# A ring of twelve slots for the expert weights, six of them in buffers of the dense stages

## What is computed

```python
mod = silu(c) @ w_ada + b_ada                      # shifts, scales, gates
h = rmsnorm(x, norm1) * (1.0 + sc1) + sh1
z = h @ w_in                                       # pool group, gates B and C, value
pool_out = pool_mixer(u, ...)                      # windows 2/4/8/16, then w_pool
conv_out = conv_mixer(gate_b, gate_c, val, ...)    # three taps
x = x + g1 * (concatenate([pool_out, conv_out]) @ w_out)
h2 = rmsnorm(x, norm2) * (1.0 + sc2) + sh2
logits = h2 @ w_router + b_router                  # 32 experts, top 4, softmax over the four
g = minimum(xb @ w_gate[e] + b_gate[e], 7); u = clip(xb @ w_up[e] + b_up[e], -7, 7)
y = ((u + 1.0) * g * sigmoid(1.702 * g)) @ w_down[e] + b_down[e]
x = x + g2 * sum over the four experts of gate * y; rmsnorm(x, final_norm)
```

## Time and profile before

| | us |
|---|---|
| median of 3 runs | 1441.77 |
| lowest and highest | 1438.84, 1443.11 |
| the profiled execution's own time | 1442.45 |
| its span in the profile | 1440.7 |
| PE busy | 1292.0 |
| DVE busy | 464.9 |
| POOL busy | 304.0 |
| ACT busy | 132.0 |

### The profile page before, as it was taken

How to read it: one execution, slowest core, us unless ns; L and a number is a source line. 1 busy time by engine, 2 the same in 40 slices (tenths; PEclk the granted TensorE clock), 3 DMA queues, 4 the chain that set the end, 5 groups by cost and what they waited for, 6 DMA issues and landing times. The chain is left out here.

```text
span 1440.7 us, 44313 instructions
## 1 busy us (share of the span) xinstructions
PE 1292.0 (90%) x19889; PEld 1004.1 (70%) x19889; DVE 464.9 (32%) x708; ACT 132.0 (9%) x270; POOL 304.0 (21%) x335
## 2 busy tenths in 40 slices
PE   4999979657999999999999999999999999999710
PEld 2777734424987887877888788788779887788600
DVE  1210153442233342322333433323323333233244
ACT  3100101200010000000010000000100000001002
POOL 4002200152012211121122111221221112211226
PEclk9999989767999999999999999999999999999955
DMA  9726820235999999999999999999999999999461
GB/s 325 220 88 231 328 105 30 89 129 218 392 410 410 408 408 410 411 412 404 410 407 403 410 398 408 406 413 417 405 409 406 411 411 412 409 413 407 194 259 69
DMA packets 88792, 479.31 MB, mean 333 GB/s; under 512 B 15235, under 2 KB 24939, under 8 KB 39061
## 3 DMA queue, kind: packets, MB, share of 16 engines
q1 hardware_dynamic: 73842, 456.59, 79.3%
q0 software_dynamic: 11840, 20.64, 3.9%
q10 hardware_dynamic: 3075, 1.58, 0.5%
HBM read 468.41 MB, written 17.84 MB: 338 GB/s over the span
## 5 line engine op out<-in xcount | busy, mean ns | idle before, releaser
L1385 PE MATMUL acc<-raw,ht 128*32 128x256 f32 x12288 | 723.6, 382 | 24.7 <-DVE ht L1219 11.5
L1385 PEld LDWEIGHTS acc<-raw,ht 128*32 128x32 f32 x12288 | 565.0, 111 | 175.0 <-issue 67.8
L1385 PE MATMUL acc<-raw,at 128*32 128x256 f32 x6144 | 347.6, 380 | 2.8 <-DVE y_sb L1234 2.8
L1385 PEld LDWEIGHTS acc<-raw,at 128*32 128x32 f32 x6144 | 275.4, 110 | 60.8 <-issue 4.7
L1120 POOL DMA_INDIRECT expert_rows<-y_sb,y_idx x96 | 118.0, 1230 | 366.6 <-ACT y_idx L1158 325.6
L1109 POOL DMA_INDIRECT rows<-h_rows,row_next x90 | 91.6, 1018 | 462.6 <-DVE row_next L1214 443.2
L1266 DVE TENSOR_TENSOR g_sb<-acc,bias_gu 128x768 f32<-128x768 f32 x32 | 30.6, 958 | 326.1 <-PE acc L1385 326.1
L1155 ACT ACTIVATE y_sb<-y_sb,table 128x256 f32<-128x256 f32 x96 | 41.9, 499 | 929.8 <-DVE y_sb L1234 929.8
L862 PE MATMUL acc<-h_t,raw 128*128 128x288 f32 (+1 forms) x512 | 120.5, 398 | 1.1 <-DVE h_t L623 1.1
L862 PEld LDWEIGHTS acc<-h_t,raw 128*128 128x128 f32 x512 | 98.5, 193 | 23.0 <-issue 2.8
L1225 DVE STREAM_TRANSPOSE at<-a_sb 128x768 f32<-128x768 f32 x32 | 51.2, 1601 | 148.8 <-PE acc L1385 148.8
(11 more groups left out here) (219 smaller groups left out, 499.9 us busy)
## 6 DMA issues: line engine op xcount, KB each, us to landing
raw<-in_w_gate SPq DMA_DIRECT2D x128, 1024.0 KB, 7.5
raw<-in_w_up SPq DMA_DIRECT2D x128, 1024.0 KB, 6.1
raw<-in_w_down SPq DMA_DIRECT2D x128, 1024.0 KB, 7.6
raw<-in_w_ada SPq DMA_DIRECT2D x24, 1024.0 KB, 14.2
raw<-in_w_in SPq DMA_DIRECT2D x8, 1024.0 KB, 14.6
picked<-expert_rows SPq DMA_DIRECT2D x4, 2048.0 KB, 9.0
raw<-in_w_out SPq DMA_DIRECT2D x4, 1024.0 KB, 5.0
x_sb<-in_x_prompt SPq DMA_DIRECT2D x1, 2048.0 KB, 9.6
```

The source lines that it names most:

```text
L1385: mm = pe.matmul(out_[b][q * TB:(q + 1) * TB, :], x[:, b, k, :], w[:, kk, q * CW:(q + 1) * CW], start=(k == 0), stop=(k == KT - 1))
```

## The change

There are two rings of six slots, each one buffer: `ring_a`, the old one, and `ring_b`, new, 6 x 2048 floats per partition. The experts' weights use all twelve slots (`XSLOTS`), chunks 0 to 5 in `ring_b` and 6 to 11 in `ring_a`, with twelve semaphores of their own; the dense chunks stay in `ring_a`. Tiles of the dense stages that had buffers of their own now lie in `ring_b`: `pooled`, `wsum` and `wpool_sb` in its first two slots, `uext`, `uext_s`, `vext`, `vext_s` and `g1_bc` in the others. `picked` and `pair` of the last block lie there too. SP issues the first twelve expert chunks in the dense block, where the tiles beneath are done with: 6 and 7; then 0 and 1; stores of h2; 2 to 5; a store; 8 to 11; the last store. In the expert stage a load waits for the product twelve before it.

```diff
+XSLOTS = 12
-        raw = [keep(f"raw{s}", [P, SLOT_F]) for s in range(SLOTS)]
+        ring_a = keep("raw", [P, SLOTS * SLOT_F])
+        raw = [ring_a[:, s * SLOT_F:(s + 1) * SLOT_F] for s in range(SLOTS)]
+        ring_b = keep("raw_b", [P, SLOTS * SLOT_F])
+        slot_of = [(ring_b, s) for s in range(SLOTS)] + [(ring_a, s) for s in range(SLOTS)]
+        def slots(n, count=1):
+            ring_, s = slot_of[n]
+            return ring_[:, s * SLOT_F:(s + count) * SLOT_F]
+        slot_loaded = [sem(f"slot_loaded{s}") for s in range(XSLOTS)]
...
+        pooled = done_first([GR, NTOK])
+        wsum = [done_first([PAST + SEQ]) for i in range(2)]
+        wpool_sb = done_first([GR, P])
+        held_at[0] = 2 * SLOT_F
+        uext = done_first([GR, PAST + SEQ])
+        uext_s = done_first([GR, DEC_B, PAST + DEC_T])
+        vext = done_first([GR, CPAST + SEQ])
+        vext_s = done_first([GR, DEC_B, CPAST + DEC_T])
+        g1_bc = done_first([D])
...
             def first(n):
-                kind, e, c = FIRST_STREAM[n]
-                sp.wait_ge(*used(DENSE_CH - SLOTS + n))
-                sp.dma_start(raw[n][:, :].rearrange("p (k n) -> p k n", k=KC), expert_src(kind, e, c))\
-                    .then_inc(raw_loaded[n], 16)
-            for n in range(SLOTS - OUT_CH):
-                first(n)
-            for t in range(TT):
+                kind, j = expert_chunk(n % (2 * MCH))
+                sp.dma_start(as_rows(slots(n)), expert_src(kind, n // (2 * MCH), j)).then_inc(slot_loaded[n], 16)
+            def store(t):
                 sp.wait_ge(h_ready, TT + t + 1)
                 sp.dma_start(h2_dram[t * P:t * P + norm_rows(t), :], h_row[t % 2][0:norm_rows(t), :])\
                     .then_inc(h2_stored[t % 2], 16)
-            for n in range(SLOTS - OUT_CH, SLOTS):
+            for n in range(SLOTS, XSLOTS - OUT_CH):
+                sp.wait_ge(*used(DENSE_CH - XSLOTS + n))
                 first(n)
+            sp.wait_ge(tp_full, TP["pm_s"] + 1)
+            for n in range(2):
+                first(n)
+            for t in range(3):
+                store(t)
+            sp.wait_ge(tp_full, TP["so0"] + 1)
+            sp.wait_ge(new_packed, 4)
+            sp.wait_ge(x1_ready, PT)
+            for n in range(2, SLOTS):
+                first(n)
+            store(3)
+            for n in range(XSLOTS - OUT_CH, XSLOTS):
+                sp.wait_ge(*used(DENSE_CH - XSLOTS + n))
+                first(n)
+            store(4)
...
                 def load(i, c):
-                    n = pos(i, c)
-                    s = ring(i, c, SLOTS)
-                    kind = "gud"[c // MCH]
-                    sp.wait_ge(mm_done, n - (SLOTS - 1))
...
+                    n, s = pos(i, c), slot_at(i, c)
+                    kind, j = expert_chunk(c)
+                    sp.wait_ge(mm_done, n - (XSLOTS - 1))
+                    sp.dma_start(as_rows(slots(s)), expert_src(kind, i - (kind == "d"), j))\
+                        .then_inc(slot_loaded[s], 16)
-                for c in range(SLOTS, 2 * MCH):
-                    load(0, c)
-                with sp.Fori(1, E) as i:
+                for c in range(XSLOTS - 2 * MCH, NCH):
+                    load(1, c)
+                with sp.Fori(2, E) as i:
...
-                    pe.wait_ge(raw_loaded[ring(i, c, SLOTS)], loaded_value(i, c))
-                    w = raw[ring(i, c, SLOTS)][:, :].rearrange("p (k n) -> p k n", k=KC)
+                    pe.wait_ge(slot_loaded[slot_at(i, c)], loaded_value(i, c))
+                    w = as_rows(slots(slot_at(i, c)))
...
-            picked = [sb(f"picked{b}", [P, 2, 2, D]) for b in range(2)]
-            pair = [sb(f"pair{b}", [P, 2, D]) for b in range(2)]
+            picked = [slots(2 * b, 2).rearrange("p (a b d) -> p a b d", a=2, b=2) for b in range(2)]
+            pair = [slots(4 + b).rearrange("p (a d) -> p a d", a=2) for b in range(2)]
```

More of the change, by code:

```diff
@@ L1 @@
+import math
 from contextlib import ExitStack
@@ L131, in hybrid_step, with done_first @@
         mix_t = h_t
[L132 to L135, removed]
         gate_b = sb("gate_b", [P, GR, NTOK])
         gate_c = sb("gate_c", [P, GR, NTOK])
-        pooled = sb("pooled", [P, GR, NTOK])
-        conv = h_t[:, GR:2 * GR, :]
-        wsum = [sb(f"wsum{i}", [P, PAST + SEQ]) for i in range(2)]
-        g1_bc = sb("g1_bc", [P, D])
+        held_at = [0]
+        def done_first(dims, rows=P):
+            n = math.prod(dims)
+            at_, held_at[0] = held_at[0], held_at[0] + n
+            assert held_at[0] <= SLOTS * SLOT_F
+            names = "abc"[0:len(dims)]
+            v = ring_b[0:rows, at_:at_ + n]
+            if len(dims) == 1:
+                return v
+            return v.rearrange(f"p ({' '.join(names)}) -> p {' '.join(names)}", **dict(zip(names, dims)))
+        pooled = done_first([GR, NTOK])
+        conv = h_t[:, GR:2 * GR, :]
+        wsum = [done_first([PAST + SEQ]) for i in range(2)]
+        wpool_sb = done_first([GR, P])
+        assert held_at[0] <= 2 * SLOT_F
+        held_at[0] = 2 * SLOT_F
[4 more added lines that the diff above has]
+        g1_bc = done_first([D])
         c_rows = g1_bc[0:NC, :]
@@ L150, in hybrid_step @@
         par_rows = sb("par_rows", [4 * GR, P])
-        wpool_sb = sb("wpool_sb", [P, GR, P])
         wr_sb = sb("wr_sb", [P, KT, E])
@@ L276, in expert_src, with as_rows @@
             return rows[e, c] if isinstance(e, int) else rows[bass.ds(e, 1), c].rearrange("a p k n -> (a p) k n")
+        def as_rows(buf):
+            return buf.rearrange("p (k n) -> p k n", n=D)
         def expert_src_plain(kind, e, c):
@@ L281, in expert_src_plain, with expert_chunk @@
             return rows[bass.ds(e, 1), c].rearrange("a p k n -> (a p) k n")
-        FIRST_STREAM = [("g", 0, c) for c in range(MCH)] + [("u", 0, c) for c in range(MCH)]
+        def expert_chunk(c):
+            return "gud"[c // MCH], c % MCH
         POOL_STEPS = 24 + 2 * Q
@@ L977, in pos, with slot_at @@
             return i * NCH + (c - MCH)
-        def ring(i, c, n):
-            return (pos(i, c) if isinstance(i, int) else pos(1, c)) % n
-        assert NCH % SLOTS == 0
+        def slot_at(i, c):
+            return pos(i if isinstance(i, int) else 1, c) % XSLOTS
+        assert NCH % XSLOTS == 0
         def loaded_value(i, c):
             if isinstance(i, int):
-                return 16 * ((DENSE_CH + pos(i, c)) // SLOTS + 1)
-            base = (DENSE_CH + pos(1, c)) // SLOTS + 1
-            return (i - 1) * (16 * NCH // SLOTS) + 16 * base
+                return 16 * (pos(i, c) // XSLOTS + 1)
+            return (i - 1) * (16 * NCH // XSLOTS) + 16 * (pos(1, c) // XSLOTS + 1)
         with ExitStack() as experts:
@@ L1418, in _ @@
                 down(E)
-        LOADS = (DENSE_CH + TOTAL) // SLOTS
+        LOADS = DENSE_CH // SLOTS
         with ExitStack() as extra:
```

2 lines of the change are left out of this document (removed).

## The result

The changed kernel takes 1444.05 us, the median of 20 runs (1441.92 to 1445.96); the kernel before, run in turn with it, takes 1441.84 (20 runs, 1437.29 to 1444.78). The ratio of the pairs is 1.0018, with a 95% interval of 1.0009 to 1.0026. That is within the 0.3% that I called no change, and the 1442.8 us forecast is 1.3 us under it. The interval excludes 1, so the change costs something: about 2 us of 1442, where twice as many slots were to help.

The account below looks back on a forecast made before the run. TensorE was taken to bound the expert stage, fed in time by six slots. Steady 0, start 0 and block end +1.0 gave 1443.45 us against the profiled 1442.45, itself 0.68 above the median: forecast 1442.8, range 1438.0 to 1447.0.

Parts of the forecast that it names:

- The steady stage: Expert products once the ring is full: twelve slots lengthen a margin nobody uses, 0 us.
- the margin: Expert stage, six slots: five products, 12.95 us, between issue and need, less the longest landing of 8.2, leave 4.75 us.
- The loss per expert: Expert stage: 1.04 us per expert lost beside GpSimd's three gathers for the next expert, not for want of buffers.
- The rival of too few slots: Expert stage: the stall is a matter of buffers, thirty experts gain 1.04 us each, -31 to 1411; chance 0.03.
- The start of the experts: First expert products: earlier and additional loads remove no wait, 0 us; first product not before 297 or after 304.
- the store of t = 0: First h2 store, behind the tail of chunks 0 and 1: lands 2 to 3 us later, buffer wanted much later, 0 us.
- the other edits: Dense tiles, picked and pair in the new ring, and 12 more semaphores: 0 us each.
- The id wait: Routing, 4.44 us wait of "taken" for row numbers: taken as 0; rival that loads cause it, -4.4 + 1.0, 1439.4, chance 0.13.
- The block end: End of the dense block: loads delay the last stores for which all engines wait, +1.0 us, ends +0.9 and +6.8.
- The rival of a slower rate: Dense block's end: loads hold back stores and routing; 4.3 us at 361 GB/s, 6.8 at 328, to 1448.6; chance 0.09.
- The signs: Trace marks of being right: same pause at gathers, expert loads at 206, 262 and 267, routing's first instruction at 286 to 288.

Follow-up runs that it names:

- Depth 6: The changed kernel, its expert-stage loads held back as by a ring of six slots, against the kernel before: 1445.74 us, ratio 1.0030.
- depth 12: The changed kernel as it is, with all twelve slots used, against the kernel before: ratios 1.0023 and 1.0018.
- depth 4: The changed kernel, its expert-stage loads issued only four products ahead, against the kernel before: 1458.51 us, ratio 1.0126.
- the control: The changed kernel with its last h2 store first and a GpSimd pause ahead of each expert's first gather, against the kernel before: 1443.8 us, ratio 0.9980.
- the changed kernel again: The changed kernel without any edit, measured a second time against the kernel before: 1444.32 us, ratio 1.0023.
- the store first: The changed kernel with the last store of h2 issued before chunks 8 to 11, against the kernel before: 1440.92 us, ratio 0.9996.
- the store on ScalarE's queue: The changed kernel with the last store of h2 issued by ScalarE, loads in their order, against the kernel before: 1445.29 us, ratio 1.0020.
- the run with two pauses: The changed kernel with its last h2 store first and GpSimd pauses ahead of each expert's second and third gathers, against the kernel before: 1413.13 us, ratio 0.9759.

## Why the prediction was right, point by point

**The steady stage at 0 us: right, and for the reason given.** Landing at most 8.8 us (8.2 before), no load among what ended idle time, 32.09 us an expert. Depth 6 and depth 12 are alike in time, and depth 4, whose three products are about as long as a landing, is the first of those tried to lose. The two halves of the argument, the margin and the pause, were both tested by their own runs.

**The loss per expert goes with the gathers: right, and shown.** It was read from a pause that stands by each run of three and is missing where none is issued. A pause on GpSimd takes most of it away in either ring, and the control brings it back. The rival of too few slots is refuted: depth 12 keeps the loss, and six slots lose it when the gathers are spread. The gap that repeats once an expert looked like the consistent bubbles of which the Trainium skill, "Perfetto Trace Analysis", section Identifying Performance Opportunities, says that they can mean too few buffers; in this kernel they don't, by the ratios of depth 6 and depth 12 (1.0030 and 1.0023).

**The start of the experts, the store of t = 0, the other edits, at 0 us: nothing speaks against them.** The first product starts at 300.92, in the interval I gave, released by ht as before; in the run of the changed kernel again, whose dense part kept pace, it is at 303.93, just inside the bound of 304, by the longer block end. With the block end's cost taken out the kernel is at a ratio of 0.9996, so together the three are worth nothing that shows. None was tried by itself.

**The id wait at 0 us: right, and the runs show its cause.** The rival held that the traffic of the loads caused the 4.44 us. That traffic is gone (share 0.23) and the wait is 4.42; it is 4.44 in the kernel of six slots whose loads had gone early. The pauses on GpSimd stand in the loop of every three gathers, the first ones beside this wait too. The same instruction with the pause ahead of the third, of the second and the third, and of the first gather:

```profile
291.32 0.16 DVE L1259 TENSOR_TENSOR taken<-acc,taken 128x3 f32<-128x3 f32 x1 [3.04 <-PE acc L1425]
```

```profile
292.29 0.16 DVE L1259 TENSOR_TENSOR taken<-acc,taken 128x3 f32<-128x3 f32 x1 [1.73 <-PE acc L1425]
```

```profile
289.98 0.16 DVE L1259 TENSOR_TENSOR taken<-acc,taken 128x3 f32<-128x3 f32 x1 [0.44 <-PE acc L1425]
```

It falls from 4.42 to 3.04 and 1.73 us, and to 0.44 where the first gather comes only at 290.08, behind it. So the gathers cause it, by way of PE, whose small products DVE waits for. Not all of it comes back: with the second and the third of these edits ht waits 0.90 and 0.85 us for the rows instead.

**The block end at +1.0 us: the mechanism was right, the term was mis-sized.** It measured 3.6 us by the rows (289.51 against 285.89) and 3.4 by the medians (with the store first and without). It is also between the bounds of 0.9 and 6.8, but the value taken was the low end. The step that was off is the sum 261.7 + 22.5 + 2.5 = 286.7, which is 9.2 MB at 408 GB/s and a small transfer behind them, for SP alone. By the trace's events of the changed kernel again, the last load was down at 286.23, 24.5 us after 261.7 and not 22.5, and the store of h2 2.8 us behind it, at 289.05, when SP passed its wait. So 2.0 of the 2.4 us that the sum lacks are the time of the traffic, 0.3 the small transfer.

Besides, I followed one queue only. At the end of the block GpSimd too has to see its own stores down: in the run of the changed kernel again its last one was issued at 279.88, took 6.9 us to 286.8, and its drain ended at 288.87, 2.1 us behind the landing (the same 2.1 lie between them in the executions of before, 282.80 to 284.90, and with the store first). With the 2.6 us of the run with the store first it would have been down at 282.5 and free at 284.6, just inside the 285.4 that PE sets. The two chains end 0.2 us apart, so mending one alone gains little, as the store on ScalarE's queue showed; in the first execution of the changed kernel it was GpSimd's drain that ended last, at 286.21, against 285.93 for SP. The rival of a slower rate had the side of it right: the mean rate was below the 408 I took, 383 GB/s from 262 to 281 in this run. At its bound of 361 it would have cost 4.3 us, at 328 GB/s 6.8; it was 3.6.

**The signs.** The loads of experts were to appear at 206, 262 and 267; in the run of the changed kernel again the second and third group are at 261.36 and 267.25, and in the profiled execution of the change all are some 3 us sooner (202.81, 258.70, 264.60). Routing's first instruction was to come at 286 to 288. The profiled execution of the change has it at 286.50, which looks like a hit and isn't quite one: its dense part ran 3 us sooner. In the run whose dense part kept pace it is at 289.51. What tells is the wait itself, 4.77 and 5.12 us against 1.16.

**Why the time was near all the same.** Forecast and median are 1.3 us apart. The block end cost 2.5 us more than forecast. Scatter of the part before it is of the same size: the changed kernel's profiled executions take 1442.76 us with a granted clock of 1.00 in the first 62 us, and 1445.22 with 0.94. So the closeness of the number is partly luck; the terms are what was tested.

## What to carry to other kernels

Before making a ring deeper, set the thinnest margin (products between issue and need, times the product's time, less the longest landing) beside the engine's idle list: with both pointing away from the loads, depth is worth nothing, and the repeating gap wants another cause. When large loads are moved ahead of a barrier, follow every queue that must drain at it, and give each small store the latency it has among loads, not the one it has alone; put the small stores first. And where TensorE pauses with "issue" as the only reason, look at what GpSimd issues at that moment: spreading its indirect transfers here gave 1.7 to 2.8%, many times what the change moved.

## What the runs showed of the hardware

**Indirect transfers in a row hold TensorE.** Three issues of GpSimd 1.3 us apart cost TensorE two pauses of 0.55 to 0.59 us, though the profile names no wait between them. With 2.4 us before the third, one pause of 0.34 us is left; with 2.4 us before the second too, none by the gathers. The scatters of an expert do the same: where the first of the three takes 1.79 us, so that the second starts 2.1 us behind it, there is a pause of up to 0.4 us or none; in the one expert of each execution whose scatters stand 1.3 to 1.4 us apart (839.38, 840.75, 842.06 in the run with two pauses) there are two more, of 0.58 and 0.60, and 0.57 and 0.56 in the changed kernel. Beside 20 writes in a row 49.9 us pass from the first expert's start to the second's; with a pause after every second write 27.0, with the clock higher as well. By which path the one engine holds the other no run here shows, nor whether the number of transfers or their spacing decides.

**A small store among large loads.** With the last of eight loads of 1 MB still on their way, 8 KB took 5.5 us to land, 32 KB took 6.9 and 128 KB 8.5 and 9.0; without them 1.9, 2.6 and 2.6. The queue made a difference to the last: 6.0 us from ScalarE's, in which no load stood ahead of it.
